# Loading the first layer's input by columns: what it does to a two-layer attention and convolution kernel

## What is computed

```python
def rms_norm(x, g):
    xf = x.astype(jnp.float32)
    y = xf * lax.rsqrt(jnp.mean(xf * xf, axis=-1, keepdims=True) + RMS_EPS)
    return (y * g.astype(jnp.float32)).astype(x.dtype)

def moba_mixer(hn, w_in, w_out):
    proj = hn @ w_in                      # 2048 x 8192
    q, k, v, z = jnp.split(proj, 4, axis=-1)
    q, k, v = apply_rope(to_heads(q)), apply_rope(to_heads(k)), to_heads(v)
    o = moba_attention(q, k, v)...
    return (o * jax.nn.silu(z)) @ w_out

def conformer_mixer(hn, w_in, b_in, w_dw, b_dw, ln_g, ln_b, w_out, b_out):
    proj = hn @ w_in                      # 2048 x 6144
    u = a * jax.nn.sigmoid(g)             # a, g: the first 4096 columns + b_in
    u = causal depthwise convolution of u with w_dw (31 taps) + b_dw
    u = jax.nn.silu(layer_norm(u, ln_g, ln_b))
    return (u * jax.nn.silu(z)) @ w_out + b_out
```

## Time and profile before

| what | value |
|---|---|
| runs (3) | median 840.91 us, 840.15 to 842.20 us |
| profiled execution | 840.53 us, its span 838.7 us |
| mean granted TensorE clock | 0.998 |
| PE busy | 829.1 us, 99% |
| DVE busy | 713.2 us, 85% |
| ACT busy | 426.4 us, 51% |
| POOL busy | 342.9 us, 41% |
| DMA | 161.62 MB, mean 193 GB/s; 312 and 322 GB/s in the first two fortieths of the span |

### The profile page before, as it was taken

The page is one execution under the profiler, slowest core; times in us unless marked ns, Lnnn a source line. Parts: engine busy times, 40 slices in busy tenths (PEclk is TensorE's granted clock), DMA queues, the critical chain, the costliest instruction groups (busy, mean ns, idle before and its releaser), DMA issues.

```text
span 838.7 us, 10949 instructions
## 1 busy us (share of the span) xinstructions
PE 829.1 (99%) x3807; PEld 686.5 (82%) x3807; DVE 713.2 (85%) x1234; ACT 426.4 (51%) x589; POOL 342.9 (41%) x173
## 2 busy tenths in 40 slices
PE   9999999999999999999999999999999999999996
PEld 6888888888888888888888888888888888888884
DVE  5688799988999799979847649999999999898655
ACT  6744535455444744454446574444444454574542
POOL 0343005500441004500000298888888878894001
PEclk9999999999999999999999999999999999999999
DMA  9956556656567555746555485556555646667523
GB/s 312 322 167 204 183 154 188 192 169 200 152 188 214 180 166 156 228 165 250 173 184 198 149 295 191 179 189 200 191 167 193 200 152 200 201 219 244 192 98 100
DMA packets 97945, 161.62 MB, mean 193 GB/s; under 512 B 3348, under 2 KB 38772, under 8 KB 97396
## 3 DMA queue, kind: packets, MB, share of 16 engines
q1 hardware_dynamic: 97860, 161.13, 59.4%
q10 hardware_dynamic: 48, 0.02, 0.0%
HBM read 159.04 MB, written 2.10 MB: 192 GB/s over the span
## 4 chain that ended last, share of the span: by engine, by line
PE 97%; DMA 1%; SPq 1%; DVE 0%; issue 0%; ACT 0%; DVEq 0%; POOL 0%
PE acc L460 29%; PE acc L461 29%; PE acc L462 29%; DMA raw<-in_w_in 1%; PE acc L445 1%; PE acc L447 1%; PE acc L446 1%; PE X L461 1%; PE X L460 1%; PE X L462 1%; PE X L470 1%; PE acc L779 0%; PE acc L778 0%; PE acc L780 0%; PE X L587 0%; PE X L586 0%
## 5 line engine op out<-in xcount | busy, mean ns | idle before, releaser
L807 ACT ACTIVATE w_hi<-raw 128x1024 fp32r<-128x1024 f32 x282 | 298.6, 1060 | 340.0 <-PE acc L462 326.5
L460 PE MATMUL acc<-w_hi,xT_hi 128*128 128x512 f32 x864 | 338.7, 392 | 0.3 <-DVE w_lo L1110 0.3
L462 PE MATMUL acc<-w_hi,xT_lo 128*128 128x512 f32 x864 | 336.5, 389 | 0.0
L461 PE MATMUL acc<-w_lo,xT_hi 128*128 128x512 f32 x864 | 336.3, 389 | 0.0
L1110 DVE TENSOR_TENSOR w_lo<-raw,w_hi 128x1024 fp32r<-128x1024 f32 x180 | 242.3, 1363 | 70.1 <-ACT w_hi L807 67.8
L1607 POOL TENSOR_TENSOR w_lo<-raw,w_hi 128x1024 fp32r<-128x1024 f32 x102 | 248.3, 2442 | 45.3 <-ACT w_hi L807 44.8
L462 PEld LDWEIGHTS acc<-w_hi,xT_lo 128*128 128x128 f32 x864 | 162.2, 188 | 34.0
L460 PEld LDWEIGHTS acc<-w_hi,xT_hi 128*128 128x128 f32 x864 | 162.3, 188 | 33.5 <-issue 0.5
L461 PEld LDWEIGHTS acc<-w_lo,xT_hi 128*128 128x128 f32 x864 | 162.3, 188 | 32.8
L1400 DVE SCALAR_TENSOR_TENSOR X<-u_pad,taps,X 128x256 f32<-128x256 f32 x464 | 183.7, 480 | 3.5 <-ACT X L1020 3.5
L1570 POOL TENSOR_TENSOR small<-small 128x1 f32<-128x1 f32 (+1 forms) x7 | 4.3, 618 | 220.7 <-DVE small L1327 122.9
(11 more groups left out here) (165 smaller groups left out, 798.6 us busy)
## 6 DMA issues: line engine op xcount, KB each, us to landing
raw<-in_w_in SPq DMA_DIRECT2D x78, 1024.0 KB, 5.3
raw<-in_w_in SPq DMA_DIRECT2D x66, 512.0 KB, 4.5
raw<-in_w_out SPq DMA_DIRECT2D x32, 1024.0 KB, 5.1
gpost<-in_post_g SPq DMA_DIRECT2D x2, 1024.0 KB, 5.8
brow<-in_b_in SPq DMA_DIRECT2D x1, 2048.0 KB, 10.2
out<-xrow SPq DMA_DIRECT2D x6, 256.0 KB, 2.7
xrow<-in_x SPq DMA_DIRECT2D x4, 256.0 KB, 5.8
raw<-in_w_in SPq DMA_DIRECT2D x4, 256.0 KB, 4.7
```

Source lines behind the costliest of these rows:

```text
L460: nc.tensor.matmul(a, hi[:, k, rows], w_hi[:, slot, i], start=(k == 0), stop=False)
L461: nc.tensor.matmul(a, hi[:, k, rows], w_lo[:, slot, i], start=False, stop=False)
L462: last = nc.tensor.matmul(a, lo[:, k, rows], w_hi[:, slot, i], start=False, stop=(k == KT - 1 or n == pause))
L807: nc.scalar.activation(w_hi[:, slot], raw[:, u % LOADS, 2 * half:2 * half + 2], ACT.Copy).then_inc(hi_ready[slot], 1)
```

## The change

A copy of x in column order (for each of the 128 partitions 16 tiles of 256 rows) is handed in by the host beside x itself, as are the gains and biases by columns (`vectors`) and the taps by columns (`tap_cols`); the host only reorders.

- SP loads `x_col` in seven pieces of 1, 1, 2, 2, 2, 4 and 4 tiles (1, 2 or 4 KB per partition) in place of the row pieces. The identity and the taps come behind the rotation tables, and x by rows (2 MB) comes as one DMA behind weight load 8.
- PE makes no transposes of x, gains, biases or taps in layer 0. It runs eight matmuls on zeros, and then the tiles.
- ACT and DVE take hi and lo of x from `x_col` in SBUF.
- The row sums of squares: ACT squares `x_col` in eight batches of 128x512, two behind each of `high(10)` to `high(13)`, into two buffers in turn. POOL adds the batches up in `sq_sum` (one copy, seven additions). PE, after slice 10, waits for the last addition and sums over the partitions with four matmuls against a constant of -0.5. DVE, after `low(14)`, makes the mean of it, POOL the root.
- ACT writes the first q out after `high(14)`, where it was after `high(11)`, and DVE turns it after `low(17)` to `low(20)`.

```diff
@@ constants
+X_CHUNKS = ((0, 1), (1, 2), (2, 4), (4, 6), (6, 8), (8, 12), (12, KT))
+COLUMN_SQUARES_AT = {10: (0, 1), 11: (2, 3), 12: (4, 5), 13: (6, 7)}
+ROWS_LOAD_AT = 8
+COLUMN_MEAN_AT = 10
+EVICT_Q = 11
+FIRST_EVICT_Q, FIRST_TURN_Q = 14, 17
...
@@ SP
-            def x_load(first, last):
-                c = slice(first * SEQ, (last + 1) * SEQ)
-                sp.dma_start(xrow[:, :, c], xv[:, :, c]).then_inc(x_in[x_chunk(first)], 16)
...
+            def col_load(i):
+                a, b = X_CHUNKS[i]
+                sp.dma_start(x_col[:, a:b], x_cols[:, a:b]).then_inc(col_in[i], 16)
+            col_load(0)
             w_load(0, 0, 0, tile_in[0])
+            col_load(1)
             w_load(0, 1, 1, tile_in[1])
-            x_load(1, 1)
+            col_load(2)
             w_load(0, 2, 2, tile_in[2])
             w_load(0, 3, 3, raw_ready[0])
-            x_load(2, 2)
+            col_load(3)
             w_load(1, 0, 1, half_in)
-            x_load(3, 3)
+            col_load(4)
             w_load(1, 2, 3, raw_ready[1])
-            x_load(4, 5)
+            col_load(5)
             load(S_QKVZ, 0, 32, 2, w_in0[0], 0)
-            x_load(6, 7)
+            col_load(6)
             load(S_QKVZ, 0, 32, 3, w_in0[0], 0)
             load(S_QKVZ, 0, 32, 4, w_in0[0], D)
-            for v, rows, src in ((V_BA, 2 * KT, b_in), (V_BDW, KT, b_dw), (V_LNG, KT, ln_g), (V_LNB, KT, ln_b)):
-                sp.dma_start(vec_rows[v - NPRE:v - NPRE + rows, :], src.rearrange("l (t c) -> (l t) c", c=P)
-                             ).then_inc(vec_in, 16)
             sp.dma_start(cos_t[:], rope_cos).then_inc(rope_in, 16)
             sp.dma_start(sin_t[:], rope_sin).then_inc(rope_in, 16)
             sp.dma_start(mask[:], causal).then_inc(rope_in, 16)
-            sp.dma_start(dw_rows[:], w_dw[0].rearrange("k (t c) -> (k t) c", c=P)
-                         .rearrange("(q r) c -> r q c", r=DW_ROWS)).then_inc(dw_in, 16)
+            sp.dma_start(ident[:], identity).then_inc(ident_in, 16)
+            sp.dma_start(taps[:], tap_cols).then_inc(taps_in, 16)
             for j in range(5, 16):
                 load(S_QKVZ, 0, 32, j, w_in0[0], (j // 4) * D)
+                if j == ROWS_LOAD_AT:
+                    sp.dma_start(xrow[:], xv).then_inc(x_in, 16)
...
@@ PE
-                tile_products(0)
-                input_T(0, 1)
-                tile_products(1)
-                tile_products(2)
-                input_T(0, 2)
-                tile_products(3)
-                input_T(0, 3)
+                for t in range(2 * FINE):
+                    tile_products(t)
                 for h in range(FINE, SLICES):
...
-                    if h + 2 < SLICES:
-                        input_T(0, h + 2)
+            def column_mean():
+                pe.wait_ge(col_sum, SLICES)
+                for m in range(MT):
+                    for i in range(2):
+                        last = nc.tensor.matmul(X[0][:, 2 * m:2 * m + 2], sq_sum[:, i * SEQ + m * P:i * SEQ + (m + 1) * P],
+                                                m_half, start=(i == 0), stop=(i == 1))
+                last.then_inc(col_mean, 1)
...
-            keep_clock(4)
-            pe.wait_ge(ident_in, 16)
-            pe.wait_ge(pre_in, 16)
-            nc.tensor.transpose(X[3][:, 0:NPRE], pre_rows[:], ident[0:NPRE, 0:NPRE]).then_inc(vec_T, 1)
-            keep_clock(3)
-            input_T(0, 0)
-            keep_clock(2)
+            keep_clock(8)
             first_block()
...
-                    if s == 9 and first:
-                        pe.wait_ge(vec_in, 16 * 4)
-                        nc.tensor.transpose(X[1][:, 0:NVEC], vec_rows[:], ident[0:NVEC, 0:NVEC])
-                        pe.wait_ge(dw_in, 16)
-                        for q in range(4):
-                            last = nc.tensor.transpose(X[0][:, q * DW_ROWS:(q + 1) * DW_ROWS], dw_rows[:, q, :],
-                                                       ident[0:DW_ROWS, 0:DW_ROWS])
-                        last.then_inc(vec_T, 1)
+                    if s == COLUMN_MEAN_AT and first:
+                        column_mean()
                     if s == SCORES_AT:
-                        if first:
...
@@ ACT
+            def column_high(h):
+                act.wait_ge(col_in[col_chunk(2 * h)], 16)
+                for t in (2 * h, 2 * h + 1):
+                    last = nc.scalar.activation(xT_hi[:, t], x_col[:, t], ACT.Copy,
+                                                scale=vec[:, V_PRE0 + t:V_PRE0 + t + 1])
                 last.then_inc(xhi_ready, 1)
...
+            act.dma_start(vec[:], vectors).then_inc(vec_in, 16)
+            act.wait_ge(const_set, 2)
+            nc.scalar.activation(small[:, 112:114], m_half, ACT.Copy)
+            act.wait_ge(vec_in, 16)
...
-                if h in SQUARES_AFTER:
-                    n = SQUARES_AFTER.index(h)
-                    wait_columns(n // 2)
-                    input_squares(junk0[:], n // 2, n % 2, n)
-            for n in range(len(SQUARES_AFTER), SLICES):
-                wait_columns(n // 2)
-                input_squares(junk0[:], n // 2, n % 2, n)
+            def column_squares(n):
+                if n >= 2:
+                    act.wait_ge(col_sum, n - 1)
+                nc.scalar.activation(sq[n % 2][:], x_col[:, 2 * n:2 * n + 2].rearrange("p t r -> p (t r)"), ACT.Square
+                                     ).then_inc(ssq_ready, 1)
...
-                    if s == 12 and first:
-                        act.wait_ge(vec_T, 2)
-                        nc.scalar.activation(vec[:, NPRE:NPRE + NVEC], X[1][:, 0:NVEC], ACT.Copy)
-                        nc.scalar.activation(taps[:], X[0][:, 0:TAPS * KT], ACT.Copy).then_inc(vec_ready, 1)
-                    if s == 11:
+                    if first:
+                        for n in COLUMN_SQUARES_AT.get(s, ()):
+                            column_squares(n)
+                    if s == (FIRST_EVICT_Q if first else EVICT_Q):
...
@@ DVE
-            mean_of_parts(8, 1)
+            def column_mean():
+                dve.wait_ge(col_mean, 1)
+                sums = X[0][:, 0:2 * MT].rearrange("p (m c) -> p m c", c=2)[:, :, 0]
+                nc.vector.tensor_scalar(mean_sq, sums, -2.0 / D, RMS_EPS, ALU.mult, ALU.add).then_inc(ms_ready, 1)
...
+                    if s == COLUMN_MEAN_AT + RING and first:
+                        column_mean()
                     if not first:
                         group_end(s, g - 1)
-                    if s in range(TURN_Q, TURN_Q + 4):
-                        if s == TURN_Q:
+                    turn_q = FIRST_TURN_Q if first else TURN_Q
...
@@ POOL
+            for n in range(SLICES):
+                pool.wait_ge(ssq_ready, n + 1)
+                if n == 0:
+                    nc.gpsimd.tensor_copy(sq_sum[:], sq[0][:]).then_inc(col_sum, 1)
+                else:
+                    pool.wait_ge(col_sum, n)
+                    nc.gpsimd.tensor_tensor(sq_sum[:], sq_sum[:], sq[n % 2][:], ALU.add).then_inc(col_sum, 1)
```

More of the change, by code:

```diff
@@ L299, in units, with col_chunk, units_T, of_tile_x @@
             return SLICES + (RING * m + h + 1 if h < RING else RING + h + 1)
-        def x_chunk(h):
-            return h if h < 4 else 2 + h // 2
+        def col_chunk(t):
+            return next(i for i, (_, end) in enumerate(X_CHUNKS) if t < end)
+        def units_T(h, m):
+            return units(h, m) - SLICES
         def of_tile(t, even, pair, count):
             return (even, t // 2 + 1) if t % 2 == 0 else (pair, count)
+        def of_tile_x(t, count):
+            return (tile_xhi[t // 2], 1) if t % 2 == 0 else (xhi_ready, count)
         def loaded(first, it, per, s):
@@ L652, in _ @@
                     pe.wait_ge(ulo_ready, NG)
+                    pe.wait_ge(ident_in, 16)
                     row_T(0, 0)
@@ L1130, in input_low, with column_low @@
                         out=xT_lo[:, t], in0=X[n % 4][:, c * SEQ:(c + 1) * SEQ],
-                        scalar=vec[:, vcol + t:vcol + t + 1], in1=xT_hi[:, t].bitcast(f32),
+                        scalar=vec[:, V_PRE1 + t:V_PRE1 + t + 1], in1=xT_hi[:, t].bitcast(f32),
                         op0=ALU.mult, op1=ALU.subtract)
+                last.then_inc(xlo_ready, 1)
+            def column_low(h):
+                dve.wait_ge(xhi_ready, h + 1)
+                for t in (2 * h, 2 * h + 1):
+                    last = nc.vector.scalar_tensor_tensor(
+                        out=xT_lo[:, t], in0=x_col[:, t], scalar=vec[:, V_PRE0 + t:V_PRE0 + t + 1],
+                        in1=xT_hi[:, t].bitcast(f32), op0=ALU.mult, op1=ALU.subtract)
                 last.then_inc(xlo_ready, 1)
```

143 lines of the change are left out of this document (62 added, 81 removed).

## The result

The kernel is slower: 848.52 us median (four runs, 847.48 to 849.46) against 841.50 for the kernel before (four runs, 840.15 to 842.20), a ratio of 1.0095 (95% interval 1.0083 to 1.0107): under 1%, but clear of the noise. The forecast was 845.2: right direction, 3.3 us short. The profiled execution took 849.31 us with a span of 847.5, 8.8 us longer than before.

A forecast was written before the change was run, and what follows sets the result against it. PE's own work plus its start was taken to bound the kernel (busy 99%). Savings of 2.4 us against a 6.1 us wait, 0.45 and 0.2 gave +4.3: 844.9 by the profile, 845.2 for the median, range 840.3 to 849.

The forecast's parts named there:

- The sum: All terms added to the profiled 840.53 us: -0.9 - 1.09 - 0.42 + 6.1 + 0.45 + 0.2 = +4.3 us.
- the wait: After slice 10, PE waits for POOL's last addition of squares from T + 8.16 to T + 14.3: 6.1 us.
- the fall of the clock: Rival, chance 0.20: PE's clock falls to 1.2 GHz in the wait after slice 10 and returns slowly; 847.6 us.
- load 2: Weights of slices 4 and 5: larger x pieces let them land earlier, so slice 4 starts 0.9 us sooner (0 to 1.7).
- the small matmuls: Four matmuls on PE after slice 10 summing squares over partitions: 0.35 plus 0.1 for the pass, +0.45 us.
- the slow start: DMAs run at 278 GB/s from 2 to 10 us, against 391 after; blamed on 1 KB pieces, 2.3 us lost.
- loads 3 to 5 come before they are needed: Slices 4 to 7: these weight loads cost no wait, as load 5 has less ahead of it; no term.
- T: The end of slice 7 on PE, forecast at 30.7 us; later times are counted from it.
- Transposes, biases and taps: PE's three transpose groups in slices 4 to 7 go, -1.09 us; the gap between slices 9 and 10 shrinks, -0.42.
- the hand count: POOL's copy, seven additions and four lows between them, counted from T - 0.25, end at T + 14.2.
- The rival in which POOL keeps up: Additions and DVE's lows overlap, so PE waits only 2.0 us after slice 10; 841.0 us, chance 0.20.
- Lows behind q's turns: DVE's lows of slices 18 to 21 come late behind q's turns, 0 to 1.5 us, taken as +0.2.

## Why the prediction was right and wrong

**The step that failed.** The sum let everything behind the wait run at the full clock; the fall of the clock stood only as a rival, at 0.20. It cost 3.4 us. With it two terms were mis-sized, load 2 (-0.9, measured 0) and the small matmuls (+0.45, measured 0.8 to 0.9 at the full clock). The wait itself, which the prediction called the term that decides, came as forecast.

**Load 2, -0.9: wrong in size.** Arrival gained 0 in the profiled run (hi at 18.32, before 18.27) and 0 to 0.6 in the eight others of the same queue and the same pieces (17.63 to 18.30). The cause given for the slow start, pieces of 1 KB, is refuted by the kernel with x in such pieces. That PE would wait at slice 4 was forecast; not priced was that the clock falls behind that wait in some runs (1.5 to 2.3 us of waiting with whole loads, 0.3 before). And "loads 3 to 5 come before they are needed" was wrong for load 5: `high(10)` waited 1.81 for it and started at T - 2.1, not T - 2.4.

**Transposes, biases and taps, -1.09 and -0.42: right**, -1.37 in all with an arrival 0.06 later.

**The wait, +6.1: right.** 5.8, from additions of 1.30 and 2.1 by whether a low is under way, and an end at T + 13.9 (45.68 less 31.75) where the hand count had T + 14.2. Small errors cancel in it: load 5 made the chain 0.3 late, the copy ended only 0.47 behind the low that held it, where 0.75 was taken (its row of 1.13 is mostly waiting), and four lows held the additions by 0.8 each, not 1.0. The rival in which POOL keeps up is out.

**Four small matmuls, +0.45: wrong**, 1.73. The profile has eight for four, fp32 with two columns; they cost 0.8 to 0.9 at the full clock and twice that at the half.

**Clock: the rival that was given 0.20 came in**, on top of the forecast's own terms: +2.54 on slice 11 and 0.9 on the small matmuls, 3.4 in all where it had been priced at 2.4. The rows at the start had shown both levels, so it had grounds for more than 0.20. The kernel with matmuls on zeros in the wait has the same late sums without the fall, and its span is 3.6 us shorter. Of the four runs the two with a mean clock of 0.992 took 849.3 and 849.5, the two with 0.994 took 847.5 and 847.7; only one of the first two has a trace. With the terms at their measured sizes (load +0.9, small matmuls +1.3, clock on slice 11 +2.5, wait -0.3, lows -0.2) the profile's sum of 844.9 becomes 849.1, and the profiled execution took 849.3.

**Lows behind q's turns, +0.2: 0 here, but by luck of the wait.** The kernel in which PE adds two squares has q's turns at the same slice and its rotation ended at about the same time (58.1 for 58.7), without the stop of PE, and there PE waits 0.2 and 1.7 us for lows. In the kernels without a wait of over 1 us at the sums, this stretch bounds: their scores start 1.7 to 4.6 us later than before.
